# Moving the squares of a layer's norm beside the last FFN outputs, and multiplying the first two FFN units tile by tile

## What is computed

```python
def rms_norm(x, g):
    xf = x.astype(jnp.float32)
    y = xf * lax.rsqrt(jnp.mean(xf * xf, axis=-1, keepdims=True) + EPS)
    return (y * g).astype(x.dtype)

def modulate(x, g, shift, scale):
    return rms_norm(x, g) * (1.0 + scale[:, None, :]) + shift[:, None, :]

def swiglu(h, w_in, w_out):
    a, b = jnp.split(h @ w_in, 2, axis=-1)
    return (jax.nn.silu(a) * b) @ w_out

# in each layer, latent stream xl (and the context stream xc in layer 0 only):
    pl = jnp.split(modulate(xl, g_mix[l], sh1, sc1) @ w_in[l], IN_OFFSETS, axis=-1)
    ...                      # three head groups: neighbourhood attention, mLSTM, latent attention
    xl = xl + gt1[:, None, :] * mix_l
    xl = xl + gt2[:, None, :] * swiglu(modulate(xl, g_ffn[l], sh2, sc2), w_ffn_in[l], w_ffn_out[l])
```

## Time and profile before

| | us |
|---|---|
| median of 3 runs | 2357.04 (2356.33 to 2357.92) |
| the profiled execution | 2357.41 |
| its span | 2355.6 |
| PE busy | 2082.0 |
| DVE busy | 1181.4 |
| ACT busy | 749.4 |
| POOL busy | 635.1 |
| idle of PE before L1116, all four norms | 71.3, released by DVE L1754 |
| idle of PE before L1011 (hhi products) | 36.1, of it 14.6 released by DVE L1774 |

### The profile page before, as it was taken

How to read it: one execution, slowest core, us unless ns; L and a number is a source line. 1 busy time by engine, 2 the same in 40 slices (tenths; PEclk the granted TensorE clock), 3 DMA queues, 4 the chain that set the end, 5 groups by cost and what they waited for, 6 DMA issues and landing times.

```text
span 2355.6 us, 29264 instructions
## 1 busy us (share of the span) xinstructions
PE 2082.0 (88%) x11392; PEld 1710.9 (73%) x11392; DVE 1181.4 (50%) x2112; ACT 749.4 (32%) x1208; POOL 635.1 (27%) x820
## 2 busy tenths in 40 slices
PE   1776899989989799999999967788989887999999
PEld 0565788866667588888888864677866665878887
DVE  1554643357885566346616555564457874211112
ACT  2232223255663311111111132332264653222222
POOL 0111021121011233333333412113131103555555
PEclk9888999999998799999999988999899998999999
DMA  7200143110000143323323311001011001332333
GB/s 271 75 27 19 38 161 108 37 36 27 10 19 26 37 143 108 99 99 108 118 80 108 108 47 36 19 29 54 28 45 36 19 9 46 97 98 90 98 97 100
DMA packets 76239, 165.53 MB, mean 70 GB/s; under 512 B 5192, under 2 KB 46664, under 8 KB 75088
## 3 DMA queue, kind: packets, MB, share of 16 engines
q1 hardware_dynamic: 75728, 163.28, 20.9%
q10 hardware_dynamic: 384, 0.47, 0.1%
HBM read 161.63 MB, written 2.10 MB: 70 GB/s over the span
## 4 chain that ended last, share of the span: by engine, by line
PE 76%; DVE 11%; ACT 5%; issue 4%; DMA 1%; POOL 1%; SPq 1%; PEld 0%; PEldq 0%; DVEq 0%; ACTq 0%; POOLq 0%
PE psum L1011 21%; PE psum L1013 21%; PE psum L1012 21%; DMA marope<-c_rope 1%; PE psum L1540 1%; DVE naptlo L1877 1%; PE psum L1062 1%; POOL wlo L499 1%; DVE n_t L1754 1%; PE psum L1093 1%; PE psum L1180 1%; DVE n_t L1782 1%; DVE hlo L1774 1%; PE psum L1309 1%; PE psum L1295 1%
## 5 line engine op out<-in xcount | busy, mean ns | idle before, releaser
L499 POOL TENSOR_TENSOR wlo<-raw,whi 128x256 fp32r<-128x256 f32 x816 | 634.9, 810 | 1712.6 <-ACT whi L525 1712.6
L1011 PE MATMUL psum<-hhi,whi 128*128 128x512 f32 (+1 forms) x1640 | 592.2, 361 | 36.1 <-DVE hlo L1774 14.6
L1012 PE MATMUL psum<-hlo,whi 128*128 128x512 f32 (+1 forms) x1640 | 583.6, 356 | 0.0
L1013 PE MATMUL psum<-hhi,wlo 128*128 128x512 f32 (+1 forms) x1640 | 583.5, 356 | 0.0
L525 ACT ACTIVATE whi<-raw 128x1024 fp32r<-128x1024 f32 x204 | 215.4, 1059 | 943.1 <-PE psum L1013 942.4
L1011 PEld LDWEIGHTS psum<-hhi,whi 128*128 128x128 f32 x1640 | 316.3, 193 | 92.6 <-issue 22.9
L1013 PEld LDWEIGHTS psum<-hhi,wlo 128*128 128x128 f32 x1640 | 315.6, 192 | 43.4
L1012 PEld LDWEIGHTS psum<-hlo,whi 128*128 128x128 f32 x1640 | 316.6, 193 | 40.3
L2306 DVE TENSOR_TENSOR ffuf<-ffsa,psum 128x768 f32<-128x768 f32 (+1 forms) x44 | 36.1, 821 | 348.8 <-ACT ffsa L968 348.8
L2291 DVE SCALAR_TENSOR_TENSOR ffmacc<-wm,csil,ffmacc 128x256 f32<-128x256 f32 x336 | 189.7, 605 | 10.1 <-DVE ffmacc L2291 4.9
L1011 PE MATMUL psum<-uhi,whi 128*128 128x512 f32 (+1 forms) x528 | 189.0, 358 | 2.6 <-DVE ulo L2310 1.5
(11 more groups left out here) (305 smaller groups left out, 3408.2 us busy)
## 6 DMA issues: line engine op xcount, KB each, us to landing
raw<-w_stream SPq DMA_DIRECT2D x204, 512.0 KB, 3.6
wm<-w_mod SPq DMA_DIRECT2D x80, 512.0 KB, 3.9
wm<-w_mod SPq DMA_DIRECT2D x8, 1024.0 KB, 18.3
xres<-x_t SPq DMA_DIRECT2D x8, 384.0 KB, 6.6
out<-xres SPq DMA_DIRECT2D x8, 256.0 KB, 2.4
consts<-c_f SPq DMA_DIRECT2D x1, 353.0 KB, 7.8
narpb<-rpb ACTq DMA_DIRECT2D x2, 120.0 KB
mlmask<-c_gate ACTq DMA_DIRECT2D x2, 108.0 KB
```

The costliest lines, as they stand in the source:

```text
L499: ins = nc.gpsimd.tensor_tensor(wlo[:, q % 2, c:c + UW // 4], raw[:, q % RAW, c:c + UW // 4], whi[:, q % 2, c:c + UW // 4], ALU.subtract)
L1011: mm(dst, ah, bh, start=first, stop=False)
L1012: mm(dst, ah, bl, start=False, stop=False)
L1013: return mm(dst, al, bh, start=False, stop=last)
```

## The change

1. The squares of layer 1's first norm move into the last output group of layer 0's FFN. ACT rounds the weights up to unit k + 2, waits for `x_free` of tile k and squares it; DVE adds the square of tile m - 1 behind the residual update of tile m, and that of tile 7 behind the loop. `mod_take` and `mod_mix` go behind tile 5. Since the usual buffers are in use there, this norm takes the FFN's `uf` and `sa` for its squares and sums (`norm_bufs`). The transfer of the bias table `rb` is issued by ACT at the start of layer 1's norm instead of its end.
2. The first two units of each FFN (slice j = 0, a and b) are multiplied by a new function `ff_first`: for each tile k it waits for `h_lo` and does all column ranges of both units, then goes to the next tile. Both units are released together at the end. In layer 0 the second range of a lies in bank 6, so the first SiLU is in two parts.

```diff
+        def norm_bufs(l, which):
+            if l and not which:
+                return FF["uf"], FF["sa"]
+            return NRM["sq"], NRM["t"]
@@ ACT @@
+            def square_of(l, which, full, k):
+                n0, q0 = 16 * l + 8 * which, 0 if full else CTX_LEN
+                if k >= 2:
+                    act.wait_ge(sq_used, n0 + k - 1)
+                A(norm_bufs(l, which)[0][:, k % 2, q0:], xres[:, k, q0:], ACT.Square).then_inc(sq_done, 1)
...
-                for k in range(KT):
+                tb = norm_bufs(l, which)[1]
+                if l and not which:
+                    small(NA["rb"][:, :], rpb[l])
+                for k in range(KT if l == 0 or which else 0):
...
-                    if k >= 2:
-                        act.wait_ge(sq_used, n0 + k - 1)
-                    A(NRM["sq"][:, k % 2, q0:], xres[:, k, q0:], ACT.Square).then_inc(sq_done, 1)
+                    square_of(l, which, full, k)
...
                         act.wait_ge(w_used, u + 2)
                         act.wait_ge(ff_free, l * HG + j + 1)
-                        A(FF["sa"][:, par, q0:], ff_psum(par, 0, full), ACT.Silu).then_inc(ff_sa, 1)
+                        if full and j == 0:
+                            A(FF["sa"][:, 0, 0:512], bank(0), ACT.Silu)
+                            A(FF["sa"][:, 0, 512:TOK], bank(6)[:, 0:256], ACT.Silu).then_inc(ff_sa, 1)
+                        else:
+                            A(FF["sa"][:, par, q0:], ff_psum(par, 0, full), ACT.Silu).then_inc(ff_sa, 1)
                         his(min(u + 6, b + 2 * n + 2))
                     his(u0(l, FF_OUT[g]) + 4)
-                    his(u0(l, FF_OUT[g]) + KT + (2 if g < len(FF_GROUPS) - 1 else 0))
+                    if full and g == len(FF_GROUPS) - 1:
+                        for k in range(KT):
+                            his(u0(l, FF_OUT[g]) + k + 3)
+                            act.wait_ge(x_free, 2 + l * XPL + (2 + g) * KT + k + 1)
+                            square_of(l + 1, 0, True, k)
+                    else:
+                        his(u0(l, FF_OUT[g]) + KT + (2 if g < len(FF_GROUPS) - 1 else 0))
@@ PE @@
-            def ff_in_unit(u, par, ab, full, tiles=None):
+            def ff_in_unit(u, par, ab, full):
...
-                        if tiles is not None and i == 0:
-                            pe.wait_ge(h_lo, tiles + k + 1)
...
+            def ff_first(l, full):
+                u = u0(l, FF0)
+                if full:
+                    parts = ((0, 0, 512, bank(0)), (0, 512, TOK, bank(6)[:, 0:256]),
+                             (1, 0, 256, bank(1)[:, 256:512]), (1, 256, TOK, bank(2)))
+                else:
+                    parts = ((0, CTX_LEN, TOK, bank(0)), (1, CTX_LEN, TOK, bank(1)))
+                w = (unit(u), unit(u + 1))
+                for k in range(KT):
+                    pe.wait_ge(h_lo, 16 * l + KT + k + 1)
+                    for ab, r0, r1, dst in parts:
+                        (wh, wl), c = w[ab], P * k
+                        ins = mm3(dst, wh[:, c:c + P], wl[:, c:c + P], hhi[:, k, r0:r1], hlo[:, k, r0:r1], k == 0, k == KT - 1)
+                ins.then_inc(w_used, 2)
...
-                        for ab in range(2):
-                            ff_in_unit(b + 2 * (j - j0) + ab, j % 2, ab, full,
-                                       tiles=16 * l + KT if j == ab == 0 else None)
+                        if j == 0:
+                            ff_first(l, full)
+                        else:
+                            for ab in range(2):
+                                ff_in_unit(b + 2 * (j - j0) + ab, j % 2, ab, full)
@@ DVE @@
             def add_square(l, which, full, k):
...
-                acc = NRM["t"][:, 0, q0:]
+                sq, tb = norm_bufs(l, which)
+                acc = tb[:, 0, q0:]
...
                 if which:
                     add_square(l, which, full, KT - 1)
-                else:
+                elif l == 0:
                     for k in range(KT):
                         add_square(l, which, full, k)
...
                         ins.then_inc(x_free, 1)
                         if l == 0 and m == 1 and g < len(FF_GROUPS) - 1:
                             mod_product(MODN(j0 + n) - 1)
+                        if full and g == len(FF_GROUPS) - 1:
+                            if m:
+                                add_square(l + 1, 0, True, m - 1)
+                            if m == 5:
+                                mod_take(1, 0, MODC, bank(7))
+                                mod_mix(1, 0)
+                                mod_mix(1, 1)
                     j0 += n
-                if l == 0:
-                    mod_take(1, 0, MODC, bank(7))
-                    mod_mix(1, 0)
-                    mod_mix(1, 1)
+                if full:
+                    add_square(l + 1, 0, True, KT - 1)
```

More of the change, by code:

```diff
@@ L587, in norm_phase @@
                     for r0, r1 in rr:
-                        ins = A(hhi[:, k, r0:r1], NRM["t"][:, k % 2, r0:r1], ACT.Identity,
+                        ins = A(hhi[:, k, r0:r1], tb[:, k % 2, r0:r1], ACT.Identity,
                                 bias=mods[:, l, 24 * which + k, cls(r0):cls(r0) + 1])
@@ L593, in na_inputs @@
             def na_inputs(l):
-                small(NA["rb"][:, :], rpb[l])
+                if l == 0:
+                    small(NA["rb"][:, :], rpb[l])
                 act.wait_ge(w_used, u0(l, NA_V) + 2)
@@ L1115, in norm_phase @@
                 for r0, r1 in ranges(full):
-                    ins = mm(psum_pair(psum, 3)[:, r0:r1], ones, NRM["t"][:, 0, r0:r1], start=True, stop=True)
+                    ins = mm(psum_pair(psum, 3)[:, r0:r1], ones, norm_bufs(l, which)[1][:, 0, r0:r1], start=True, stop=True)
                 ins.then_inc(st_done, 1)
@@ L1753, in add_square @@
                     dve.wait_ge(sq_used, n0 + k)
-                    V.tensor_tensor(acc, acc, NRM["sq"][:, k % 2, q0:], ALU.add).then_inc(sq_used, 1)
+                    V.tensor_tensor(acc, acc, sq[:, k % 2, q0:], ALU.add).then_inc(sq_used, 1)
                 else:
-                    V.tensor_copy(acc, NRM["sq"][:, 0, q0:]).then_inc(sq_used, 1)
+                    V.tensor_copy(acc, sq[:, 0, q0:]).then_inc(sq_used, 1)
             def norm_phase(l, which, full):
@@ L1773, in lower @@
                     for r0, r1 in rr:
-                        ins = V.scalar_tensor_tensor(hlo[:, k, r0:r1], NRM["t"][:, k % 2, r0:r1],
+                        ins = V.scalar_tensor_tensor(hlo[:, k, r0:r1], tb[:, k % 2, r0:r1],
                                                      mods[:, l, 24 * which + k, cls(r0):cls(r0) + 1],
@@ L1781, in norm_phase @@
                     for r0, r1 in rr:
-                        ins = V.scalar_tensor_tensor(NRM["t"][:, k % 2, r0:r1], xres[:, k, r0:r1],
+                        ins = V.scalar_tensor_tensor(tb[:, k % 2, r0:r1], xres[:, k, r0:r1],
                                                      amix[:, l, which, k, cls(r0):cls(r0) + 1],
```

## The result

The changed kernel takes 2344.47 us, the median of 3 runs (2339.7 to 2346.0), against 2357.04: a ratio of 0.9942, 95% interval 0.9919 to 0.9965, 12.6 us faster. Six further runs of it, beside 17 of the kernel before (median 2356.78, 2347.97 to 2359.97), gave 2344.83 and 0.9950 (0.9935 to 0.9965). The profiled execution took 2344.47 with a span of 2342.7, 12.9 us shorter than before.

A forecast was written before the change was run, and what follows sets the result against it. TensorE, busy 88% of the span, was taken as the bound; 9.1 (squares) + (4.6 - 1.7) (layer 0's FFN) + (-1.4 - 1.7) (layer 1's) = 8.9 us gain, from 2357.04 to 2348.1, range 2342.5 to 2353.

The forecast's parts named there:

- Part 1, behind the last output: Start of layer 1: only two additions (2.93 us) stay before the sums over the squares, idle 4.2 instead of 13.29, gain 9.1.
- Part 1, beside the outputs: Layer 0's last FFN outputs: added squares, additions and modulation steps fit the 6.24 us output period and cost nothing.
- Part 2, the first pair: First two units of each FFN: dense tile work, 18.5 us in layer 0 and 12.8 in layer 1, without gaps.
- the cold start: Start of each FFN's first pair: low clock for 3.7 us, costing 1.85 us.
- Part 2, the stall: Before each FFN's third unit: new 4.4 us wait for GpSimd; third unit 4.6 sooner in layer 0, 1.4 later in layer 1.
- The clock behind the stall: Dense work after each FFN's new wait: window clock near 0.79, 1.7 us lost each time, with 0 and 2.9 as ends.
- (a): Rival: nothing lost after the two FFN waits and layer 1's sums over squares run fast; 2343.3 us, chance 0.25.
- (b): Rival: 2.9 us lost instead of 1.7 after each FFN wait, cold starts last 5.8 us; 2352.6 us, chance 0.15.
- (d): Rival: dense tiles do not raise the clock in the first FFN pairs; net 15.0 us slower, 2372 us, chance 0.05.
- (c): Rival: layer 1's squares run only behind the last output, gaining nothing, tile order nets -0.2; 2357.2 us, chance 0.05.

The follow-up runs named there:

- part 1 alone: The changed kernel with the old function for the first two FFN units put back, squares still moved: 2341.46 us, and 2340.78 us when run again.
- the kernel with lags 3 and 5: The changed kernel with unit b 3 tiles behind unit a in layer 0, 5 in layer 1, each released at its own end: 2338.24 us, ratio 0.9926.

## Why the prediction was right

**The direction and the size.** 2344.47 lies in the range of 2342.5 to 2353 and 3.5 us under the forecast of 2348. The sum had 8.9 us; its own terms delivered 11.1; the rest of the 12.6 is stages I and IV and the runs' scatter, which is chance and not the forecast's merit.

**Part 1, behind the last output: right in mechanism, the sizes off by 1.5 us.** I priced the two additions at 2.93 by layer 0's FFN norm, because GpSimd works in both places. They took 2.34: the second 1.29 as there, the first 0.97 instead of 1.55. In the new order square 6 is long done, so the first addition starts at 1374.44, with the end of the update and just ahead of GpSimd (1374.58); in the FFN norm it waits for its square and starts behind GpSimd (775.08 against 774.39). Whether that is why it was quick no run here separates. The idle was 3.59 and not 4.2. And the sums found the higher clock for half their time (0.75, 1.90 us), which I had kept as a bound. That was this execution's luck: behind the same idle of 3.59 they took the full 2.90 in two of the experiments, as forecast, and 1.53 in two others. Term by term: 9.7 instead of 9.1, and 0.9 instead of 0.

**Part 1, beside the outputs: right.** Squares, additions and modulation steps cost nothing there: the updates span 40.06 us as before, and stage II with part 1 alone is 588.7 and 589.1 against 588.6.

**Part 2, the first pair: right.** 806.3 - 787.9 = 18.4 us for layer 0, where I had 18.5; the cold start was low for 3.0 us instead of 3.7. In layer 1 it was 12.6 us, where I had 12.8.

**Part 2, the stall: right.** 4.22 and 4.14 us where I had 4.4, released by GpSimd, in both layers. The third unit came 4.9 us sooner in layer 0 (I had 4.6) and 1.0 later in layer 1 (1.4).

**The clock behind the stall: right, and shown.** Both windows read 0.79, 1.7 us each. Filled with idle matmuls they read 1.00 and 1.6 us came back in each FFN. The Trainium skill, "TensorE: Matmul & The Clock Gate", section "HAM oscillation — how this bites in real kernels", tells of waits that come back with every tile, with each next tile starting cold. Here a single wait in each FFN is paid in the same way, 1.7 us at either stall. The trace differs in one point: in layer 0 the unit behind the wait started at 1.00 and fell to 0.50 only 0.85 us later, while in layer 1 it started low.

**The rivals.** (a) had one of its two halves: the sums ran faster, the stalls did not. (b) fell with the 0.79 behind the stalls and the 3.0 us at the low clock at the start of the pairs, (d) with those pairs, continuous and at the full clock after 3 us. (c) fell with the idle of 3.59.

**What the forecast said only in passing,** under (c): that the tile order as a whole is worth nothing (-0.2 in my numbers, 1.0008 measured), so that all of the gain is part 1's. With the release taken apart the tile order does pay: 6.3 us in stage II against the old order, and 0.5 in V, in the kernel with lags 3 and 5.

## What to carry to other kernels

Working several double-buffered units together releases them together, and then the whole refill lies open behind them; let one run ahead of the other by just the refill's length. An idle of TensorE inside dense work can cost more than its length: behind 4.2 us it was 1.6 to 1.7 us more here, once 2.4, so count both. It need not: the window at 267.60 in the kernel before read 1.00. Where executions scatter by several us, keep a ledger between marks that all kernels have: it settled stage by stage what the medians could not. A median 4 us off its ledger needs a neutral edit beside it, in the same series, before it is believed.

## What was not expected of the hardware

The kernel before had three runs within 1.6 us, but 17 runs later spread from 2347.97 to 2359.97. And with a neutral swap of two column ranges a median was 2346.1 instead of 2340.8 and 2341.5, while the one stage that it touches stayed within 0.3 us (II: 588.7 and 589.1, then 589.0). Matmuls whose results nobody reads, 32 of 256 columns, were enough to hold the full clock through a wait.
